# Last attention pair among the first state group's products, late sums one unit later, output projection by seven products

## The chip, the cores and the metric

One core of one Trainium2 chip runs the whole program in one launch. The metric is the device time of that core in microseconds, the median of several executions, lower is better. The kernel before takes 2818.53 us (three executions, 2817.77 to 2819.26).

## The reference

256 tokens of width 2048 (and 256 context tokens) pass two blocks. The first block has two layers, each with an RMS norm whose shift, scale and gate come from a small product of a condition vector with `ada_w` (2048 x 6144 per layer). What matters here is layer 0 and the norm behind it, cut to its lines:

```python
shift, scale, gate = adaln(c, ada_w[i], ada_b[i])
h = modulate(rms_norm(x, norm_g[i]), shift[:, None], scale[:, None])
p = h @ w_in                        # q, gate, z, k, v, and x, B, C, dt of the state space part
ya = neighbourhood_attention(q, k, v, kc, vc, rpb) * silu(gate_a)     # 16 heads
yb = gated_group_rmsnorm(bidirectional_ssd(lat, con, a) + d * x_lat, z, ssm_norm_g)   # 8 groups
out = concatenate([ya, yb]) @ w_out            # 4096 x 2048
x = x + gate[:, None] * out
```

All of it is float32. The second layer (a short convolution) and the second block (two more attentions) follow and are not touched, except that their first product waits for the norm of the new x.

## The kernel before, in words

Features lie on partitions: `hT` holds the normed tokens (256 own, 256 context) as 16 chunks of 128 features, `yT` the mixer's output, `xT` the residual. Weights come in tiles of 2048 rows by 256 columns (2 MB) into four slots `w[0..3]`, requested by SyncE in program order (`load`), each once `acc_full` says that TensorE has finished with the slot.

**Stages.** (1) Eight attention pairs (two heads each, `na(i)`), (2) eight state groups (`ssd(g)`), (3) the output projection (`out`) in eight tiles of 256 columns, then the next norm and the `sc` phase of layer 1.

**Seven products.** A tile's product is a 2 x 2 block product (two halves of the 2048 features, two halves of columns, two halves of tokens). Most phases do it with seven block products in place of eight (Strassen-Winograd): VectorE makes sums of token quarters once (`token_sums`) and of weight quarters for each tile (`sums_one` and `sums_two` in the attention, `weight_sums` from `sc` on: four subtractions of 128 x 1024 each), TensorE makes 7 x 8 matmuls of 128 x 128 instead of 16 x 2 of 128 x 256, ScalarE copies the seven blocks from PSUM to `staged`, and VectorE puts them together in six small additions (`na_combine`, `combine`). The state groups and the output projection use plain products. There `out_half` multiplies the first half of `yT` (the attention's output, the 2048 rows of weight slot 2*cb) or the second (slot 2*cb+1) into `bank[cb]`; `add_out` adds the bank, times the gate, to `xT`.

**A pair.** TensorE's program (`na` in the tensor block, L737) has six units of seven products each (`na_unit`: q, gate, k, k of the context, v, v of the context), and between them the scores, transposes and values of the pair before, a = i - 1 (`na_scores`, `na_transposes`, `na_values`), and three sums of squares (`na_sums`). Every engine runs its own program in order, so a wait holds up all that stands behind it.

**Late parts and late sums.** What `ada_w` still has to give (the gate of layer 0, all of layer 1) is computed beside the pairs. GpSimd fetches 1 MB pieces into a ring of two places (`late_chunks`; piece c is requested when VectorE has taken piece c - 2), VectorE multiplies and adds each into `aacc` (`late_part(i, c)`, four instructions of 128 x 512, eight parts per pair), then TensorE adds up the partitions with eight two-column matmuls (`late_sums(i)`, the last thing of a pair, waits for `late_taken` of all eight parts), and VectorE takes them into `mod` (`late_mod`).

**The last pair.** Its scores, transposes and values have no next pair to lie in: they stand by themselves after `na(7)` (TensorE, for h in range(2)), with softmax and transposed copies on VectorE between. The position biases of pair 7 (`na_biases(7)`: four small gathers on SyncE, a mask addition on VectorE, L1767) are requested inside `ssd(0)`, behind the loads of slots 0 and 1. Then comes `ssd(0)`: X in two column halves (`featured(..., 0, 0)` and `(..., 0, 1)`, 16 matmuls of 512 columns each), between them `steps_of_dt` (64 matmuls of 64 columns), then `sums_of_dt`, B, C, Z and the transposes.

The order of each engine's program is written out by hand.

## Time and profile before

| | us |
|---|---|
| median of three executions | 2818.53 |
| the profiled execution, its own time | 2821.06 |
| its span in the trace | 2818.9 |
| TensorE matmul busy | 2734.9 (97%) |
| TensorE weight load busy | 2363.3 |
| VectorE busy | 1548.2 (55%) |
| ScalarE busy | 466.4 (17%) |
| mean of what the DMA queues moved | 160 GB/s |

The page gives busy time per engine over the span. A matmul of the program shows as two records in the trace (float32), so a product of eight matmuls is x16 there. PEclk is the granted TensorE clock as a share of 2.4 GHz: 0.50 is 1.2 GHz. "idle before <- releaser" tells how long the engine stood still before an instruction and what ended that.

### The profile page before, as it was taken

Reading aid. Unit: us, or ns where it says so; the run is one execution under the profiler, and the core shown is the slowest. Engines: PE = TensorE matmul, PEld = TensorE weight load, DVE = VectorE, ACT = ScalarE, POOL = GpSimd, SP = SyncE. Lnnn points to the kernel's source line nnn. Section 1 sums busy time; section 2 is a strip of 40 time slices with the busy share of each in tenths; the row PEclk is TensorE's granted clock in tenths of the full one; section 3 lists DMA queues with packets and bytes.
Section 4 is the critical chain, followed back from the end, with each engine's and each line's share of the span. In section 5 each row is a group of like instructions: output and inputs, shape, how many; then the busy total and the mean of one; then the engine's idle time right before and its main releaser. Section 6 shows DMA issues by size and latency. Waiting matters only on the chain. (4 is left out here: it accounts for less than half of the span.)

```text
span 2818.9 us, 44137 instructions
## 1 busy us (share of the span) xinstructions
PE 2734.9 (97%) x18608; PEld 2363.3 (84%) x18608; DVE 1548.2 (55%) x2733; ACT 466.4 (17%) x915; POOL 51.2 (2%) x72
## 2 busy tenths in 40 slices
PE   7999999999996999999999999999999999999999
PEld 1498999999995666666668888999999899999999
DVE  3686676776673245555554004565666665555543
ACT  0221111121211122222221001111111111121211
POOL 0000000000000000000000000000000000000000
PEclk9999999999997999999999999999999999999999
DMA  9765665566545233333333554555554544445442
GB/s 383 284 201 166 201 203 180 175 219 194 169 135 174 73 105 105 104 104 104 104 104 105 179 168 149 162 180 161 166 178 158 172 148 139 144 150 160 157 137 87
DMA packets 380515, 450.07 MB, mean 160 GB/s; under 512 B 20452, under 2 KB 351704, under 8 KB 379480
## 3 DMA queue, kind: packets, MB, share of 16 engines
q1 hardware_dynamic: 351232, 354.86, 40.0%
q0 software_dynamic: 19520, 75.50, 7.5%
q10 hardware_dynamic: 9624, 17.68, 1.7%
q8 instruction: 109, 1.79, 0.3%
q14 instruction: 30, 0.25, 0.0%
HBM read 441.66 MB, written 6.36 MB: 159 GB/s over the span
## 5 line engine op out<-in xcount | busy, mean ns | idle before, releaser
L556 PE MATMUL bank<-hT,w 128*128 128x128 f32 (+2 forms) x6144 | 1017.9, 324 | 6.1 <-ACT hT L1200 4.6
L556 PEld LDWEIGHTS bank<-hT,w 128*128 128x128 f32 x6144 | 801.1, 195 | 191.6 <-issue 181.9
L556 PE MATMUL bank<-yT,w 128*128 128x128 f32 (+1 forms) x3872 | 569.8, 308 | 1.7 <-DVE yT L2038 1.0
L556 PEld LDWEIGHTS bank<-yT,w 128*128 128x128 f32 x3872 | 531.3, 191 | 33.4 <-DVE yT L2038 1.2
L1200 ACT ACTIVATE work<-bank 128x512 f32<-128x512 f32 (+2 forms) x298 | 153.9, 525 | 1210.6 <-PE bank L556 1205.7
L556 PE MATMUL bank<-hT,work 128*128 128x128 f32 x2352 | 279.5, 275 | 0.0
L556 PEld LDWEIGHTS bank<-hT,work 128*128 128x128 f32 x2352 | 270.9, 192 | 0.0
L556 PEld LDWEIGHTS bank<-w,hT 128*128 128x128 f32 x1792 | 245.0, 191 | 20.8 <-issue 5.7
L556 PE MATMUL bank<-w,hT 128*128 128x128 f32 (+2 forms) x1792 | 261.4, 305 | 0.7 <-DMA work<-in_ssd_d 0.7
L1782 DVE SCALAR_TENSOR_TENSOR work<-xT,silc,work 128x512 f32<-128x512 f32 x240 | 180.4, 752 | 76.9 <-DMA xT<-in_ada_w 69.8
L1200 ACT ACTIVATE work<-work 128x512 f32<-128x512 f32 (+3 forms) x299 | 168.5, 569 | 275.7 <-DVE work L1935 150.3
L556 PE MATMUL bank<-work 128*128 128x256 f32 (+2 forms) x400 | 118.0, 416 | 23.5 <-issue 18.7
L556 PEld LDWEIGHTS bank<-w,yT 128*128 128x128 f32 x1024 | 116.9, 192 | 3.8 <-issue 3.8
L2093 DVE TENSOR_TENSOR work<-yT 128x128 f32<-128x128 f32 x37 | 10.8, 293 | 195.8 <-ACT yT L1200 195.8
L556 PE MATMUL bank<-w,yT 128*128 128x128 f32 x1024 | 118.2, 275 | 0.0
L2093 DVE TENSOR_TENSOR work<-work 128x128 f32<-128x128 f32 x40 | 11.7, 292 | 170.8 <-ACT work L1200 170.8
L556 PEld LDWEIGHTS bank<-work 128*128 128x128 f32 x400 | 71.1, 196 | 34.3 <-issue 22.1
L2118 DVE SCALAR_TENSOR_TENSOR xT<-bank,mod,xT 128x256 f32<-128x256 f32 x16 | 7.0, 480 | 166.3 <-PE bank L556 166.3
L1935 DVE SCALAR_TENSOR_TENSOR work<-work,colp 128x512 f32<-128x512 f32 (+1 forms) x128 | 87.6, 685 | 15.1 <-DVE work L1933 0.9
L2081 DVE TENSOR_TENSOR w<-w 128x1024 f32<-128x1024 f32 x77 | 94.3, 1225 | 2.6
L556 PE MATMUL bank<-w,work 128*2 128x512 f32 (+1 forms) x192 | 76.0, 551 | 9.8 <-DMA w<-in_ada_w 9.8
L1933 DVE TENSOR_SCALAR work<-work,colp 128x512 f32<-128x512 f32 (+1 forms) x32 | 16.3, 510 | 115.1 <-ACT work L1200 115.1
(190 smaller groups left out, 2224.2 us busy)
## 6 DMA issues: line engine op xcount, KB each, us to landing
w<-in_na_ssd_w_in SPq DMA_DIRECT2D x48, 2048.0 KB, 11.0
xT<-in_ada_w POOLq DMA_DIRECT2D x64, 1024.0 KB, 7.5
w<-in_sc_w_in SPq DMA_DIRECT2D x32, 2048.0 KB, 9.0
w<-in_w_in SPq DMA_DIRECT2D x32, 2048.0 KB, 9.0
w<-in_na_ssd_w_out SPq DMA_DIRECT2D x16, 2048.0 KB, 10.0
w<-in_ada_w SPq DMA_DIRECT2D x12, 2048.0 KB, 11.3
w<-in_na_ssd_w_in SPq DMA_DIRECT2D x16, 1024.0 KB, 7.7
w<-in_sc_w_out SPq DMA_DIRECT2D x8, 2048.0 KB, 8.6
```

Source lines behind the costliest of these rows:

```text
L556: return nc.tensor.matmul(dst, lhsT, rhs, start=start, stop=stop, skip_group_check=free)
L1200: return nc.scalar.activation(*args, **kw)
L1782: last = v.scalar_tensor_tensor(out=aacc[:, block, :], in0=aring[:, at, kc, :], scalar=silc[:, k:k + 1], in1=aacc[:, block, :], op0=ALU.mu ...
L1933: link(v.tensor_scalar(o, tap(0), col("conv_w0", c), col("conv_b", c), ALU.mult, ALU.add))
L1935: last = v.scalar_tensor_tensor(out=o, in0=tap(k), scalar=col(f"conv_w{k}", c), in1=o, op0=ALU.mult, op1=ALU.add)
L2081: v.tensor_tensor(quarter(s, 0, 1), quarter(s, 1, 1), quarter(s, 0, 1), ALU.subtract)
L2093: v.tensor_tensor(u[:, 0, :], p(0), p(2), ALU.add)
L2118: last = v.scalar_tensor_tensor(out=chunk(xT, k + ch), in0=bank[b % 2][:, ch * T:(ch + 1) * T], scalar=gate, in1=chunk(xT, k + ch), op0=AL ...
```

## The change

1. The last pair's attention (pair 7) goes between halves of the first state group's two X products (TensorE's `ssd`, first iteration): scores of head 0, half of X's first column half, transposes, scores of head 1, the other half; values of head 0, transposes, late sums, half of X's second, values of head 1, the rest. `steps_of_dt` follows, and `sums_of_dt` moves between the two halves of B.
2. `na_biases(7)` is requested right after the last attention weight; the weights of dt are loaded by ScalarE right after its `na(7)` with a semaphore of their own.
3. `late_sums(a)` moves from the end of pair a to behind unit 0 of the next pair; VectorE does parts 6 and 7 of a pair at the start of the next one, around `sums_two(n + 1)`, and the others each a little later.
4. Output tiles 2 to 7 are made by seven products for each half of `yT`, added up in the same PSUM blocks over both halves. VectorE makes eight token sums and eight weight differences per tile (`out_sums`), ScalarE stages seven blocks (`staging_out`), VectorE combines them (`out_combine`). Tiles 0 and 1 stay plain products, but go through ScalarE's copy. The squares for the norm get a place of their own. The weight sums of the `sc` phase's slot 1 move behind the token sums.

```diff
--- before
+++ after
@@ -241,9 +241,10 @@
+    squared = L(2, 2, T)
...
-    assert u_pad.shape and 7812 <= WORK - 3 * 8 * P
+    assert u_pad.shape and 8836 <= WORK - 3 * 8 * P
@@ -276,7 +277,7 @@
-    PHASES = [("na", 8, 12, [2, 4, 8, 12]), ("ssd", 8, 6, [2, 4, 6, 6]), ("out", 4, 2, [1, 1, 2, 2]),
+    PHASES = [("na", 8, 12, [2, 4, 8, 12]), ("ssd", 8, 6, [2, 4, 6, 6]), ("out", 4, 4, [2, 2, 4, 4]),
@@ -312,6 +313,11 @@
+    OUT_IN = (lambda a, k: halves(yT, 0, a, k), lambda a, k: halves(yT, DC, a, k))
+    OUT_SUM = [{j: hT[:, EIGHT * (n // 2):EIGHT * (n // 2 + 1), T * h + (n % 2) * P:T * h + (n % 2 + 1) * P]
+                for n, j in enumerate((1, 2, 3, 4))} for h in range(2)]
@@ -480,6 +487,7 @@
+        na_biases(7)
@@ -740,6 +746,7 @@
+                late_sums(a)
@@ -757,19 +764,13 @@
-            late_sums(i)
...
-        for h in range(2):
-            na_scores(7, h)
-            na_transposes(7, h)
-            na_values(7, h)
...
-            pe.wait_ge(ssd_in, 64)
+            pe.wait_ge(wdt_in, 16)
@@ -802,20 +803,30 @@
             dst = accumulate("ssd", 0, g)
-            featured(dst[:, :], 0, 0, T + TC).then_inc(acc_full, 1)
             if first:
+                na_scores(7, 0)
+                featured(dst[:, :], 0, 0, T + TC, None, range(EIGHT))
+                na_transposes(7, 0)
+                na_scores(7, 1)
+                featured(dst[:, :], 0, 0, T + TC, None, range(EIGHT, DC)).then_inc(acc_full, 1)
+                dst = accumulate("ssd", 1, g)
+                na_values(7, 0)
+                na_transposes(7, 1)
+                late_sums(7)
+                featured(dst[:, :], 0, 1, T + TC, None, range(EIGHT))
+                na_values(7, 1)
+                featured(dst[:, :], 0, 1, T + TC, None, range(EIGHT, DC)).then_inc(acc_full, 1)
                 steps_of_dt()
             else:
+                featured(dst[:, :], 0, 0, T + TC).then_inc(acc_full, 1)
                 pe.wait_ge(s_xtk, g)
...
                 last.then_inc(s_cb, 1)
-            dst = accumulate("ssd", 1, g)
-            featured(dst[:, :], 0, 1, T + TC).then_inc(acc_full, 1)
-            if first:
-                sums_of_dt()
-            else:
+                dst = accumulate("ssd", 1, g)
+                featured(dst[:, :], 0, 1, T + TC).then_inc(acc_full, 1)
                 pe.wait_ge(s_xe, g)
@@ -923,25 +936,44 @@
-        def out_proj(i):
...
+        for cb in range(2):
+            loaded(2 * cb + 1, "out", 0)
+            for ch in range(2):
+                last = out_half(cb, ch, 1)
+            last.then_inc(acc_full, 2)
+        def out_products(tile, half):
+            def add(dst, weights, tokens, clears):
+                for kc in range(EIGHT):
+                    last = mm(dst, weights[:, kc, :], tokens[:, kc, :], clears and half + kc == 0, half == 1 and kc == EIGHT - 1, True)
+                return last
+            s = 2 * (tile % 2) + half
+            pair = (bank[3], bank[4]) if tile % 2 == 0 else (bank[0], bank[1])
+            loaded(s, "out", tile // 2)
+            x, sums, (t1, t2, t4) = OUT_IN[half], OUT_SUM[half], [(sums_x, sums_y)[half][:, m, :, :] for m in range(3)]
+            a = lambda m: pair[0][:, m * P:(m + 1) * P]
+            b = lambda m: pair[1][:, m * P:(m + 1) * P]
+            if half == 0 and tile > 2:
+                pe.wait_ge(acc_free, BANKS["out"] + 2 * tile - 2)
+            add(a(0), quarter(s, 0, 0), x(0, 0), True)
+            add(a(1), quarter(s, 1, 0), x(0, 1), False)
+            pe.wait_ge(s_made, 12 + 4 * half)
+            pe.wait_ge(o_t, 2 * tile + half - 3)
+            add(a(3), quarter(s, 0, 1), sums[3], False)
+            last = add(a(2), t2, sums[2], False)
+            if half == 1:
                 last.then_inc(acc_full, 1)
-        iterations(pe, 4, out_proj)
+            add(b(0), t1, sums[1], True)
+            add(b(1), quarter(s, 1, 1), sums[4], False)
+            last = add(b(2), t4, x(1, 1), False)
+            last.then_inc(acc_full if half == 1 else o_half, 1)
+        for tile in range(2, 8):
+            for half in range(2):
+                out_products(tile, half)
         norm_halves(1)
@@ -1343,6 +1375,7 @@
+        act.dma_start(wdt, w_in[:, :, COL_DT:COL_DT + NDT]).then_inc(wdt_in, 16)
@@ -1469,17 +1501,39 @@
+        def staging_out(t):
+            flat = staged.rearrange("p a b -> p (a b)")
+            at = BANKS["out"] + 2 * t
+            wait(act, x_new, t)
+            if t < 2:
+                act.wait_ge(acc_full, at + 2)
+                A(flat[:, 0:4 * P], bank[t][:, :], ACT.Copy).then_inc(acc_free, 2)
+            else:
+                banks = (bank[3], bank[4]) if t % 2 == 0 else (bank[0], bank[1])
+                act.wait_ge(acc_full, at + 1)
+                A(flat[:, 0:4 * P], banks[0][:, :], ACT.Copy).then_inc(acc_free, 1)
+                act.wait_ge(acc_full, at + 2)
+                A(flat[:, 4 * P:7 * P], banks[1][:, 0:3 * P], ACT.Copy).then_inc(acc_free, 1)
...
-            for t in range(8):
-                act.wait_ge(acc_free, BANKS["out"] + t + 1)
-                square(t)
+            for t in range(9):
+                if t < 8:
+                    staging_out(t)
+                if t > 0:
+                    act.wait_ge(x_new, t)
+                    if t == 1:
+                        square(0)
+                    else:
+                        A(squared[:, (t - 1) % 2, :, :], xT[:, 2 * t - 2:2 * t, :], ACT.Square).then_inc(norm_sq, 1)
...
-                    act.wait_ge(x_new, t)
+                    act.wait_ge(x_new, 8 + t)
@@ -1857,12 +1911,14 @@
-                late_mod(a)
...
-                late_part(i, 0)
+                late_part(a, 6)
...
+                late_part(a, 7)
...
+            if not first:
+                late_mod(a)
@@ -1870,35 +1926,32 @@
-            if first:
-                late_part(i, 0)
-            else:
+            if not first:
...
-            late_part(i, 1)
+            late_part(i, 0)
...
+            late_part(i, 1)
+            sums_two(n + 3)
...
-            sums_two(n + 3)
-            late_part(i, 3)
...
+            late_part(i, 3)
...
-            late_part(i, 5)
...
-            late_part(i, 6)
-            late_part(i, 7)
+            late_part(i, 5)
@@ -1910,11 +1963,15 @@
+        late_part(7, 6)
+        na_softmax(7, 0, link)
+        late_part(7, 7)
+        na_turned(7, 0)
+        na_softmax(7, 1, link)
+        na_out(7, 0)
+        na_turned(7, 1)
...
-        for h in range(2):
-            na_softmax(7, h, link)
-            na_turned(7, h)
-            na_out(7, h)
+        na_out(7, 1)
@@ -2098,35 +2155,59 @@
-        def add_squares(t, squares):
+        def add_squares(t, squares, src=None):
...
-            return v.tensor_tensor(both, both, hT[:, ds(2 * t, 2), 0:T], ALU.add)
-        def add_out(phase, n, layer, squares):
...
+            return v.tensor_tensor(both, both, hT[:, ds(2 * t, 2), 0:T] if src is None else src, ALU.add)
+        def out_sums(tile, half):
+            s, place = 2 * (tile % 2) + half, (sums_x, sums_y)[half]
+            dve.wait_ge(w_loaded[s], loads(s, "out", tile // 2))
+            if half == 0 and tile > 2:
+                dve.wait_ge(o_half, tile - 2)
+            link(v.tensor_tensor(place[:, 0, :, :], quarter(s, 0, 1), quarter(s, 0, 0), ALU.subtract))
+            v.tensor_tensor(quarter(s, 0, 1), quarter(s, 1, 1), quarter(s, 0, 1), ALU.subtract)
+            link(v.tensor_tensor(place[:, 1, :, :], quarter(s, 1, 1), place[:, 0, :, :], ALU.subtract))
+            v.tensor_tensor(place[:, 2, :, :], quarter(s, 1, 0), place[:, 1, :, :], ALU.subtract).then_inc(o_t, 1)
+        def out_combine(t):
+            dve.wait_ge(acc_free, BANKS["out"] + 2 * t + 2)
+            p = lambda n: staged[:, n, :]
+            v.tensor_tensor(partial[:, 0, :], p(0), p(2), ALU.add)
+            link(v.tensor_tensor(u_b[:, 0, 0:P], p(0), p(1), ALU.add))
+            link(v.tensor_tensor(partial[:, 1, :], partial[:, 0, :], p(3), ALU.add))
+            v.tensor_tensor(u_b[:, 1, :].rearrange("p (a b) -> p a b", a=2), partial,
+                            p(4).unsqueeze(1).broadcast_to([P, 2, P]), ALU.add)
+            link(v.tensor_tensor(u_b[:, 0, P:T], partial[:, 1, :], p(6), ALU.add))
+            v.tensor_tensor(u_b[:, 1, 0:P], u_b[:, 1, 0:P], p(5), ALU.add).then_inc(o_c, 1)
+            dve.wait_ge(o_c, t - 1)
+        def add_out():
+            first = staged.rearrange("p a b -> p (a b)")
+            for t in range(8):
+                if t >= 2:
+                    if t < 7:
+                        out_sums(t + 1, 0)
+                    else:
+                        dve.wait_ge(o_half, 6)
+                        weight_sums("sc", 0, 0, link)
+                    out_combine(t)
...
-                    body(i, link)
-            add_squares(7, squares).then_inc(norm_sum, 1)
+                    dve.wait_ge(acc_free, BANKS["out"] + 2 * t + 2)
+                for ch in range(2):
+                    k = 2 * t + ch
+                    gate = mod[:, 0, 2 * DC + k:2 * DC + k + 1, 0:1].rearrange("p a b -> p (a b)")
+                    last = v.scalar_tensor_tensor(out=chunk(xT, k), in0=u_b[:, ch, :] if t >= 2 else first[:, ch * T:(ch + 1) * T],
+                                                  scalar=gate, in1=chunk(xT, k), op0=ALU.mult, op1=ALU.add)
+                last.then_inc(x_new, 1)
+                dve.wait_ge(x_new, t + 1)
+                if t == 0:
+                    out_sums(2, 0)
+                if t >= 2:
+                    link(add_squares(t - 1, 2, squared[:, (t - 1) % 2, :, :]))
+                if 1 <= t < 7:
+                    out_sums(t + 1, 1)
+            add_squares(7, 2, squared[:, 1, :, :]).then_inc(norm_sum, 1)
@@ -2147,7 +2228,10 @@
-        add_out("out", 4, 0, 2)
+        token_sums(OUT_IN[0], OUT_SUM[0], (0, EIGHT), link)
+        dve.wait_ge(s_y, 16)
+        token_sums(OUT_IN[1], OUT_SUM[1], (0, EIGHT), link)
+        add_out()
@@ -2158,6 +2242,7 @@
+        weight_sums("sc", 0, 1, link)
```

**TensorE, end of pair 6 and start of pair 7** (`work` is attention data and the late parts' `aacc`, `hT` and `yT` tokens and their sums, `w` weights). Before:

```order
L556 MATMUL bank<-w,hT 128x128 x8
L556 MATMUL bank<-cst,work 128x2 x8
L556 MATMUL bank<-hT,w 128x128 x16
L556 MATMUL bank<-yT,w 128x128 x32
L556 MATMUL bank<-hT,w 128x128 x8
L556 MATMUL bank<-work 128x512
L556 MATMUL bank<-work,cst 128x256
```

Changed:

```order
L562 MATMUL bank<-w,hT 128x128 x8
L562 MATMUL bank<-hT,w 128x128 x16
L562 MATMUL bank<-yT,w 128x128 x32
L562 MATMUL bank<-hT,w 128x128 x8
L562 MATMUL bank<-cst,work 128x2 x8
L562 MATMUL bank<-work 128x512
L562 MATMUL bank<-work,cst 128x256
```

The late sums (128x2 x8) have moved behind the 56 matmuls of unit 0.

**VectorE, the same place**: the bias mask (128x768), weight sums (128x1024, 128x8x128), late parts (`work<-xT,silc`) and `na_combine` of unit 0 (first row 128x128). Before:

```order
L1767 TENSOR_TENSOR work<-work,cst 128x768
L1793 TENSOR_TENSOR mod<-bank,colp 128x8
L1815 TENSOR_TENSOR w<-w 128x1024
L1816 TENSOR_TENSOR w<-w 128x8x128
L1780 TENSOR_SCALAR work<-xT,silc 128x512
L1782 SCALAR_TENSOR_TENSOR work<-xT,silc,work 128x512 x3
L1823 TENSOR_TENSOR w<-w 128x1024
L1825 TENSOR_TENSOR w<-w 128x1024
L1839 TENSOR_TENSOR work<-work 128x128
```

Changed:

```order
L1821 TENSOR_TENSOR work<-work,cst 128x768
L1869 TENSOR_TENSOR w<-w 128x1024
L1870 TENSOR_TENSOR w<-w 128x8x128
L1836 SCALAR_TENSOR_TENSOR work<-xT,silc,work 128x512 x4
L1877 TENSOR_TENSOR w<-w 128x1024
L1879 TENSOR_TENSOR w<-w 128x1024
L1836 SCALAR_TENSOR_TENSOR work<-xT,silc,work 128x512 x4
L1893 TENSOR_TENSOR work<-work 128x128
```

One late part (0 of the new pair) stood here; now two of the old pair (6 and 7) do.

**TensorE, last attention pair and the first state group** (`hT,w 128x512` is X, `wide<-cst,work` transposes, `w,hT 128x64` dt). Before:

```order
L559 MATMUL wide<-cst,work 128x128 x8
L556 MATMUL bank<-work 128x256 x4
L556 MATMUL bank<-work 128x512
L556 MATMUL bank<-work,cst 128x256
L556 MATMUL bank<-work 128x512
L556 MATMUL bank<-work,cst 128x256
L559 MATMUL wide<-cst,work 128x128 x8
L556 MATMUL bank<-work 128x256 x4
L556 MATMUL bank<-hT,w 128x512 x16
L556 MATMUL bank<-w,hT 128x64 x64
L556 MATMUL bank<-hT,w 128x512 x16
```

Changed:

```order
L562 MATMUL bank<-hT,w 128x512 x8
L565 MATMUL wide<-cst,work 128x128 x8
L562 MATMUL bank<-work 128x512
L562 MATMUL bank<-work,cst 128x256
L562 MATMUL bank<-work 128x512
L562 MATMUL bank<-work,cst 128x256
L562 MATMUL bank<-hT,w 128x512 x8
L562 MATMUL bank<-work 128x256 x4
L565 MATMUL wide<-cst,work 128x128 x8
L562 MATMUL bank<-cst,work 128x2 x8
L562 MATMUL bank<-hT,w 128x512 x8
L562 MATMUL bank<-work 128x256 x4
```

Each softmax now has half an X product (8 matmuls) beside it; before, nothing stood between scores and transposes.

## Rows read from the trace of the kernel before

**Rows 1.** The page: chain that ended last, shares of the span by line.

```profile
PE bank L556 42%; PE wide L556 4%; PE wide L559 0%; ACT hT L1200 0%; ACT work L1200 0%; ACT rs L1200 0%; DVE ssq L2104 0%; DVE xT L2136 0%; DVE xT L2118 0%; DVE yT L2038 0%; DVE hT L2200 0%; DVE hT L2153 0%; DVE w L1988 0%; PE bank L559 0%; DVE work L2344 0%
```

**Rows 2.** Windows: stretch, length, busy PE, PEld, DVE, ACT, POOL, PEclk, DMA, GB/s.

```profile
222.36:318.80 96.44, 93.28 (x743) 89.08 (x743) 64.48 (x107) 16.57 (x32) 5.98 (x8) 0.96 0.56 179
318.80:411.92 93.12, 93.12 (x742) 89.09 (x743) 64.48 (x107) 16.07 (x31) 5.98 (x8) 0.96 0.57 185
411.92:501.77 89.85, 89.85 (x744) 85.83 (x743) 66.41 (x108) 16.56 (x32) 6.74 (x9) 1.00 0.62 204
...
873.00:917.69 44.69, 18.73 (x66) 12.24 (x64) 10.80 (x23) 3.61 (x9) 0.00 (x0) 0.66 0.51 150
...
1500.00:1600.00 100.00, 96.11 (x460) 83.40 (x459) 26.86 (x73) 8.54 (x17) 0.00 (x0) 1.00 0.43 141
```

**Rows 3.** Timeline, TensorE: late sums that waited (start, length, ..., idle before, releaser).

```profile
222.36 2.26 PE L556 MATMUL bank<-cst,work 128*128 128x2 f32 x16 [3.84 <-DVE work L1782]
318.80 3.06 PE L556 MATMUL bank<-cst,work 128*128 128x2 f32 x16 [3.15 <-DVE work L1782]
...
684.27 3.27 PE L556 MATMUL bank<-cst,work 128*128 128x2 f32 x16 [2.42 <-DVE work L1782]
779.88 3.31 PE L556 MATMUL bank<-cst,work 128*128 128x2 f32 x16 [2.32 <-DVE work L1782]
```

**Rows 4.** Timeline, VectorE: from the end of a pair to the next.

```profile
594.21 1.41 DVE L1906 SCALAR_TENSOR_TENSOR work<-work,colp 128x512 f32<-128x512 f32 x2
595.53 0.28 DVE L1839 TENSOR_TENSOR work<-work 128x128 f32<-128x128 f32 x1
...
597.37 0.96 DVE L1767 TENSOR_TENSOR work<-work,cst 128x768 f32<-128x768 f32 x1
598.25 0.16 DVE L1793 TENSOR_TENSOR mod<-bank,colp 128x8 f32<-128x8 f32 x1
598.33 1.21 DVE L1815 TENSOR_TENSOR w<-w 128x1024 f32<-128x1024 f32 x1
...
600.72 0.48 DVE L1780 TENSOR_SCALAR work<-xT,silc 128x512 f32<-128x512 f32 x1
```

**Rows 5.** Timeline, ScalarE: staging in the `sc` phase, one seven-product tile apart.

```profile
1781.36 0.49 ACT L1200 ACTIVATE work<-bank 128x384 f32<-128x384 f32 x1 [4.76 <-PE bank L556]
...
1793.86 0.49 ACT L1200 ACTIVATE work<-bank 128x384 f32<-128x384 f32 x1 [4.76 <-PE bank L556]
```

**Rows 6.** Timeline, VectorE and GpSimd: a late part that waits for its piece, five pairs.

```profile
312.48 6.27 DVE L1782 SCALAR_TENSOR_TENSOR work<-xT,silc,work 128x512 f32<-128x512 f32 x8 [7.78 <-DMA xT<-in_ada_w]
...
493.46 6.27 DVE L1782 SCALAR_TENSOR_TENSOR work<-xT,silc,work 128x512 f32<-128x512 f32 x8 [2.15 <-DMA xT<-in_ada_w]
...
571.95 0.75 POOL L418 DMA_DIRECT2D xT<-in_ada_w  x1 [7.05 <-DVE work L1782]
...
585.50 6.27 DVE L1782 SCALAR_TENSOR_TENSOR work<-xT,silc,work 128x512 f32<-128x512 f32 x8 [4.20 <-DMA xT<-in_ada_w]
...
677.58 3.12 DVE L1782 SCALAR_TENSOR_TENSOR work<-xT,silc,work 128x512 f32<-128x512 f32 x4 [6.78 <-DMA xT<-in_ada_w]
...
773.56 6.27 DVE L1782 SCALAR_TENSOR_TENSOR work<-xT,silc,work 128x512 f32<-128x512 f32 x8 [7.05 <-DMA xT<-in_ada_w]
```

**Rows 7.** Timeline, TensorE: a wait in the last state group.

```profile
1502.69 1.13 PE L556 MATMUL bank<-work 128*128 128x256 f32 x4 [1.65 <-DVE work L2064]
```

**Rows 8.** Timeline: bias request and mask of pair 7, sums of squares, dt.

```profile
858.78 1.02 PE L556 MATMUL bank<-work,cst 128*128 128x512 f32 x2
...
876.02 5.93 SPq L472 DMA_DIRECT2D work<-in_na_rpb  x4
...
892.48 0.96 DVE L1767 TENSOR_TENSOR work<-work,cst 128x768 f32<-128x768 f32 x1 [16.94 <-DMA work<-in_na_rpb]
...
932.48 14.51 PE L556 MATMUL bank<-w,hT 128*128 128x64 f32 x128 [0.68 <-DMA work<-in_ssd_d]
```

**Rows 9.** Timeline: output projection, TensorE, its last six tiles and the norm behind it.

```profile
1569.30 166.00 PE L556 MATMUL bank<-yT,w 128*128 128x256 f32 x768 [0.75 <-issue]
...
1737.73 1.13 PE L556 MATMUL bank<-ssq,cst 128*128 128x256 f32 x4 [2.42 <-DVE ssq L2104]
```

More of the change, by code:

```diff
@@ L1000, in sc @@
                 if is_first(i) and s == 0:
-                    seven("sc", s, i, H, H_SUM, (norm_out, 2 * DC), 8)
+                    seven("sc", s, i, H, H_SUM, (norm_out, 2 * DC), 16)
                 else:
@@ L1077, in sbreak @@
             if first:
-                seven("sb", 0, i, H, H_SUM, (norm_out, 3 * DC), 20)
+                seven("sb", 0, i, H, H_SUM, (norm_out, 3 * DC), 28)
             else:
@@ L1179, in rows @@
             last.then_inc(o_tr, 1)
-        pe.wait_ge(s_made, 32)
+        pe.wait_ge(s_made, 40)
         for t in range(2, 7):
@@ L2099, in combine @@
             dve.wait_ge(c_made, TILES[phase] + 4 * i + s + 1)
-        def add_squares(t, squares):
+        def add_squares(t, squares, src=None):
             dve.wait_ge(norm_sq, squares + t + 1)
             both = ssq[:, :].rearrange("p (a b) -> p a b", a=2)
-            return v.tensor_tensor(both, both, hT[:, ds(2 * t, 2), 0:T], ALU.add)
-        def add_out(phase, n, layer, squares):
-            per = PHASE[phase][2]
-            def body(i, link, ahead=None):
-                for b in range(per):
-                    if ahead and b == 1:
-                        ahead(0)
-                        ahead(1)
-                    k = i * (2 * per) + 2 * b
-                    dve.wait_ge(acc_full, BANKS[phase] + i * per + b + 1)
-                    for ch in range(2):
-                        gate = mod[:, layer, ds(2 * DC + k + ch, 1), 0:1].rearrange("p a b -> p (a b)")
-                        last = v.scalar_tensor_tensor(out=chunk(xT, k + ch), in0=bank[b % 2][:, ch * T:(ch + 1) * T],
-                                                      scalar=gate, in1=chunk(xT, k + ch), op0=ALU.mult, op1=ALU.add)
-                    last.then_inc(acc_free, 1)
-                    if not (isinstance(i, int) and i * per + b < 2):
-                        link(add_squares(i * per + b - 1, squares))
-            for i in range(n):
-                if i == n - 1:
-                    body(i, link, lambda b: weight_sums("sc", 0, b, link))
-                else:
-                    body(i, link)
-            add_squares(7, squares).then_inc(norm_sum, 1)
```

29 lines of the change are left out of this document (7 added, 22 removed).

## The prediction

> **What bounds the kernel now.** I read the page first, then the windows of the attention pairs, then the waits of TensorE, then the timeline around each wait. The chain that ended last runs almost wholly through TensorE's matmul line [rows 1], so an edit is worth what it takes from TensorE's program: matmul time, waits, or time at the lower clock. VectorE, ScalarE and the queues count only where TensorE waits for them. The reader is to see three places. First, seven attention pairs of the same work last 89.85 us when nothing disturbs them, and 93.12 or 96.44 otherwise [rows 2]. Second, the stretch after the last pair is 44.69 us long and TensorE is busy for 18.73 of it, at a mean clock of 0.66 [rows 2]. Third, the output projection is plain: its last six tiles are 768 records in 166.00 us [rows 9], 27.67 us a tile, while a seven-product tile of one weight slot takes 12.50 us (two stagings of the same form are 12.50 apart [rows 5]), which is 25.0 for the two slots of an output tile.
>
> **How the sum is made.** The profiled execution took 2821.06 us, its span is 2818.9; the median shown is 2818.53. All terms are differences read in that one execution, and I take them from the median.
>
> **Output projection.** Tiles 2 to 7 save 27.67 - 25.00 = 2.67 us each, 16.0 us in six. VectorE's new work per tile is eight subtractions of some 1.22 (as in rows 4), 9.8, with a combination of 1.84 (595.53 to 597.37 [rows 4]), additions of 0.9 and squares of 0.7: 13.3 us beside 25 of TensorE. Differences for the first half of tile t+1 are made when half 0 of tile t is done (12.5 us before they are wanted), those for the second after tile t's combination, some 9 us into tile t+1, wanted at 16. Both are covered, by 3 us or more; without that cover each missing microsecond would be paid once per tile. ScalarE gains two copies a tile, far below its limit. Tile 2 now needs only one slot to start, where TensorE waited 0.75 us for two [rows 9]: -0.75. Behind the last tile comes a copy (0.49 and a hop, 0.6) and a combination (1.84) before the additions: +2.4. This wait is already there (2.42 [rows 9]) and ends in a low clock either way. The weight sums of `sc` slot 1, now behind the token sums, take 4.9 us, while TensorE has its own last product of slot 0 and two of slot 1 (3 x 1.79 = 5.4) to do: nothing. Sum: **-14.3**. Bounds: with every difference in time and a free tail -16.7; if each tile still waits, 0.
>
> *A page weighed here.* By the rows a 256-column record costs 166.00/768 = 0.216 us and a 128-column one 12.50/112 = 0.1116. The Trainium skill ("TensorE: Matmul & The Clock Gate", section "Wait — 56ns, not 53.3ns?") puts a fixed 2.5 ns or so on every matmul, which speaks against seven small products in place of wide ones. Estimated from that page, the ratio of 128 to 256 columns is 55.8 to 109.2 ns, a tile would save 2.9 us and six 17.6; the rows show slightly more loss, and they decide.
>
> **The last attention pair.** The stretch of 44.69 us holds the late sums, two scores, two sets of transposes and two values. What these cost at full clock follows from the clean pair: 89.85 less six units of 12.50 and three sums of squares of at most 1.02 [rows 8] leaves 11.8. So 32.9 us are waits and low clock. The biggest wait goes because the biases are requested a pair earlier: now the gathers are issued at 876.02 and the mask waits 16.94 us for them [rows 8]. What is late next is the mask itself. VectorE has, after the last unit, the staging copy and hop (0.6), the combination (1.84) and the mask (0.88, 597.37 to 598.25 [rows 4]), so TensorE waits 3.3 us before its first scores. I count a fall of the clock for that: 3.3 us more (price below). Each softmax then lies beside half an X product of about 7 us (16 records of 512 columns, four times 128 x 0.1116 each: 7.1), and VectorE needs about 3 for a softmax plus 3.1 for the late part before or behind it; head 1's values stand behind another such half. Moving dt's weights ahead takes its 0.68 us [rows 8]. The sums of dt now lie inside B; their own short wait and low clock remain. Term: -32.9 + 3.3 + 3.3 - 0.7 = **-27.0**, with bounds of -31 (the clock holds, mask sooner) and -20 (half a softmax exposed twice).
>
> **Late sums one unit later.** Now TensorE waits at four of eight late sums, 3.84 + 3.15 + 2.42 + 2.32 = 11.7 us [rows 3]. After each the clock is at 1.2 GHz for a while: a pair without a wait but after one lasts 93.12 against 89.85, 3.27 more, and 96.44 - 3.15 - 89.85 gives 3.44 [rows 2, 3]. With 3.35 a time the four cost 13.4; together **25.1 us** that the move could give back.
>
> But what stands behind it? VectorE's order at the start of a pair, from TensorE's last matmul of the pair before: 0.6 (copy and hop), 1.84 (combination), 0.88 (mask), 2.39 (first weight sums, 598.33 to 600.72 [rows 4]), 3.12 (part 6, the x4 row [rows 6]), 2.4 (second weight sums), 3.12 (part 7). That is 14.4 us. TensorE reaches the late sums after one unit, 12.5. So it waits 1.9 us in each of seven pairs, even if VectorE is in time for all that went before. The old order hid this: the late sums ended one pair and two parts had been finished before it.
>
> VectorE is not in time. The piece for old part 6 lands 3.2 us before the end of its pair (312.48 against 318.80 - 3.15 [rows 6, 3]), or 8.3, 6.1, 4.3 and 4.0 before it in the other rows (493.46 against 501.77, 585.50 against 501.77 + 89.85, 677.58 against 681.85, 773.56 against 777.56 [rows 2, 3, 6]). It was requested when part 4 was taken; new part 5 is requested when part 3 is, at the same place in the pair, beside the same loads and gathers. Behind it now come its own 3.12, 2.4 of weight sums and 1.4 for k [rows 4], 6.9 us, before the pair's last combination, which could start 0.6 after the end. A piece that lands less than 6.3 before the end delays the chain: by 3.1, 0, 0.2, 2.0 and 2.3 us, mean 1.5. The wait becomes 1.9 + 1.5 = 3.4, seven times: 23.8.
>
> Does the clock fall? It did after each wait of 2.32 and more followed by the late sums [rows 3], in which the array does almost nothing; a wait of 1.65 before wide matmuls left it at 1.00 [rows 2, 7]. New waits lie between 1.9 and 5, also followed by late sums. I take six falls in seven: 20.1. Bounds: none, 0; seven, 23.5. New cost 43.9, less 25.1: **+18.8** (from -11.8 with seven waits of 1.9 and no fall, to +32 with 4.8 and seven falls).
>
> Sum: -14.3 - 27.0 + 18.8 = -22.5, so 2796 us.
>
> **Rivals.**
> (a) *Pieces come early* (0.15). Part 5 lands with time to spare, waits are 1.9 and the clock falls in five pairs: 13.3 + 16.8 - 25.1 = +5, total -36.3, 2782 us. For it: two of five landings would do it. Against it: the piece requested at 571.95 is used at 585.50, 13.6 us later, with VectorE idle for it [rows 6].
> By the Trainium skill ("DMA: Bandwidth & Descriptors", section "Anatomy of one DMA — SWDGE (gpsimd) path"), such a transfer takes about 2.0 us plus its bytes over 436 GB/s, an estimated 4.4 us for 1 MB, which would make this rival the forecast; the trace does not agree here, with 13.6 where other queues move data as well.
> (b) *The clock holds* (0.10): waits of 1.9, no fall. -11.8 in the pairs, 2765 us. For it: 1.9 is nearer to 1.65 than to 2.42. Against it: the 1.84 us of late sums behind each.
> (c) *The interleaved softmaxes are exposed* (0.08): VectorE meets late part 7 before it copies the transposes, and its order lets each head wait some 3 us, with a fall each: 2 x (3 + 3.3) = +12.6, 2809 us. For it: a late part of 3.1 stands in front. Against it: 7 us of X beside each.
> (d) *Seven products bring nothing* (0.05), because slots arrive late (two loads must land, then 4.9 us of differences, inside one tile of 25) and each tile waits 2.7 us: 2812 us. Against it: VectorE is busy for 26.86 of the 100 us in which this phase begins [rows 2].
> (e) *Slower* (0.05). VectorE's lateness at the pair's start feeds on itself: part 5's piece arrives in all pairs 3.6 us later than in the mean row, so that the wait before the late sums is 7 us. Seven times 7 + 3.35 = 72.5, less 25.1, is +47.4 against gains of 41.3: 2825 us. It decides from a wait of (41.3 + 25.1)/7 - 3.35 = 6.1 us on. Against it: the longest that the rows give is 1.9 + 3.1 = 5.0.
>
> **How the numbers follow.** The forecast has 0.57; its own range is 2786 to 2806. Below 2772 lies rival (b), above 2811 lie (e) and parts of (c) and (d), some 0.17 together: range 2772 to 2811. About 0.2% of this kernel (5.6 us) is what a measurement can tell from no change. Faster by more, under 2812.9: 0.89. Within it: 0.06. Slower: 0.05.
>
> **What would show it.** In the new trace: late sums (128x2) with an idle time before them of 1.9 to 5 us in all seven pairs and windows of pairs at 0.95 to 0.97 clock, pairs of 95 to 98 us; VectorE's part 7 as the releaser. One wait of some 3.3 us before the first scores of pair 7, then no idle over 1 us until dt; dt's matmuls begin some 47 us behind the last unit (3.3 + 11.8 + 28.6 of X + 3.3 for the clock = 47), with both X products already done. Output tiles 25.0 us apart with TensorE idle nowhere between. I am wrong if the late sums don't wait (then 2752), if pairs are shorter than 92 us, or if output tiles are above 26.

## The result, and the profile after

| | before | after |
|---|---|---|
| median of the runs (four of each) | 2818.15 | 2800.9 |
| lowest and highest | 2816.86, 2819.26 | 2798.93, 2804.05 |
| the profiled execution's own time, its span | 2821.06, 2818.9 | 2804.05, 2801.8 |
| PE busy, DVE busy, ACT busy | 2734.9, 1548.2, 466.4 | 2726.5, 1625.3, 473.9 |

The ratio is 0.9946, 95% interval 0.9929 to 0.9963: faster by 17.2 us (forecast: 22.5 faster, 2796 us, range 2772 to 2811). In the traces the change gains 41.3 us in two places and gives 24.2 of them back in the third, in waits that it lengthens and in the lower clock behind them.

The page follows the chain that ended last through the whole span, and the chain passes through VectorE and a DMA (first two lines, after). Before's page (third line) can't be set beside it: there the chain was followed back only to 1518 us, 46% of the span, so [rows 1] says nothing of the attention pairs.

```profile
PE 88%; DVE 7%; DMA 4%; issue 1%; ACT 0%; SPq 0%; DVEq 0%; POOLq 0%; ACTq 0%
PE bank L562 81%; PE wide L562 5%; DMA xT<-in_ada_w 3%; DVE work L1836 3%; DMA w<-in_ada_w 1%; PE wide L565 1%; DVE w L1877 1%; DVE w L1869 1%; DVE w L1870 1%; DVE w L1879 1%; PE bank L565 0%; DVE work L1959 0%; ACT work L1232 0%; DVE work L1896 0%; DVE work L1895 0%
```

```profile
PE 45%; DVE 0%; ACT 0%; issue 0%; DVEq 0%; ACTq 0%
```

**Late sums.** TensorE's timeline after, which answers to [rows 3]; where four of eight late sums waited before, seven do:

```profile
236.72 3.57 PE L562 MATMUL bank<-cst,work 128*128 128x2 f32 x16 [5.63 <-DVE work L1836]
334.13 3.57 PE L562 MATMUL bank<-cst,work 128*128 128x2 f32 x16 [3.68 <-DVE work L1836]
433.14 3.57 PE L562 MATMUL bank<-cst,work 128*128 128x2 f32 x16 [4.51 <-DVE work L1836]
529.51 2.18 PE L562 MATMUL bank<-cst,work 128*128 128x2 f32 x16 [1.88 <-DVE work L1836]
623.81 3.57 PE L562 MATMUL bank<-cst,work 128*128 128x2 f32 x16 [2.59 <-DVE work L1836]
719.90 1.95 PE L562 MATMUL bank<-cst,work 128*128 128x2 f32 x16 [3.06 <-DVE work L1836]
815.23 3.57 PE L562 MATMUL bank<-cst,work 128*128 128x2 f32 x16 [3.60 <-DVE work L1836]
```

The waits sum to 25.0 us (11.7 before). A pair ends 12.5 us, one unit, before such a wait begins: at 218.59, 317.95, 416.13, 515.13 and so on. The windows between these ends answer to [rows 2]; the columns are the same, and the granted clock, 1.00 in an undisturbed pair, is below it in each:

```profile
218.59:317.95 99.36, 93.72 (x744) 88.38 (x744) 66.35 (x109) 16.68 (x32) 6.74 (x9) 0.95 0.54 176
317.95:416.13 98.18, 94.50 (x744) 88.93 (x744) 63.66 (x106) 16.68 (x32) 5.24 (x7) 0.95 0.56 179
416.13:515.13 99.00, 94.49 (x744) 88.92 (x744) 67.71 (x110) 16.67 (x32) 6.75 (x9) 0.95 0.56 184
515.13:608.72 93.59, 91.71 (x744) 86.82 (x744) 63.20 (x105) 16.68 (x32) 5.99 (x8) 0.98 0.57 181
```

Length less wait less 89.85 (the undisturbed pair) is what the clock took: 3.88, 4.65, 4.64 and 1.86 in these, 24.8 us in all seven.

**Last pair.** TensorE's timeline behind the last unit (ends 897.31) answers to the 44.69 us window [rows 2] and to [rows 8]:

```profile
900.93 2.05 PE L562 MATMUL bank<-work 128*128 128x512 f32 x2 [3.62 <-DVE work L1821]
902.76 1.06 PE L562 MATMUL bank<-work,cst 128*128 128x256 f32 x2
...
906.18 7.21 PE L562 MATMUL bank<-hT,w 128*128 128x512 f32 x16
913.22 1.04 PE L565 MATMUL wide<-cst,work 128*128 128x128 f32 x8
...
926.15 1.84 PE L562 MATMUL bank<-cst,work 128*128 128x2 f32 x16
...
943.39 14.40 PE L562 MATMUL bank<-w,hT 128*128 128x64 f32 x128
```

One wait for the mask (L1821), 3.62 us, then nothing idle up to dt, 46.1 us behind the last unit. The late sums without a wait take 1.84 us.

**Output projection.** ScalarE's staging copies stand 25.01 us a tile apart (27.67 before [rows 9]), and TensorE waits nowhere inside; the norm behind waits longer than its 2.42 [rows 9]:

```profile
1689.89 0.49 ACT L1232 ACTIVATE work<-bank 128x384 f32<-128x384 f32 x1 [4.70 <-PE bank L562]
...
1714.90 0.49 ACT L1232 ACTIVATE work<-bank 128x384 f32<-128x384 f32 x1 [4.70 <-PE bank L562]
```

```profile
1536.89 31.46 PE L562 MATMUL bank<-yT,w 128*128 128x256 f32 x160 [0.97 <-DVE yT L2095]
...
1719.66 2.07 PE L562 MATMUL bank<-ssq,cst 128*128 128x256 f32 x4 [4.80 <-DVE ssq L2161]
```

**Where the 17.1 us of span went,** by the same marks in both traces:

| stretch | before | after | difference | forecast |
|---|---|---|---|---|
| start to end of pair 0 | 218.52 | 218.59 | +0.1 | 0 |
| pairs 1 to 7 | 654.48 | 678.72 | **+24.2** | +18.8 |
| end of pair 7 to behind the sums of dt | 91.33 | 64.3 | **-27.0** | -27.0 |
| first matmul of the output projection to its norm | 197.07 | 182.77 | **-14.3** | -14.3 |
| all else | | | -0.1 | 0 |

(64.3 is 968.45 - 6.87 - 897.31: half of B, 6.87 us, now lies ahead of the sums of dt and is taken off.)

### The profile page after: what moved, and what is told of

The parts are those of the page before. It is cut to its first block, busy times and chain, and to the rows that moved or that the text cites. A ratio compares the mean times of both kernels' runs of the same rounds, so it can differ in the third digit from the quotient of the medians.

```text
span 2801.8 us, 45408 instructions
## 1 busy us (share of the span) xinstructions
PE 2726.5 (97%) x19184; PEld 2370.1 (85%) x19184; DVE 1625.3 (58%) x2825; ACT 473.9 (17%) x929; POOL 51.2 (2%) x72
## 2 busy tenths in 40 slices
DMA packets 380523, 450.19 MB, mean 161 GB/s; under 512 B 20452, under 2 KB 351704, under 8 KB 379480
## 3 DMA queue, kind: packets, MB, share of 16 engines
q1 hardware_dynamic: 351232, 354.86, 41.3%
## 4 chain that ended last, share of the span: by engine, by line
PE 88%; DVE 7%; DMA 4%; issue 1%; ACT 0%; SPq 0%; DVEq 0%; POOLq 0%; ACTq 0%
PE bank L562 81%; PE wide L562 5%; DMA xT<-in_ada_w 3%; DVE work L1836 3%; DMA w<-in_ada_w 1%; PE wide L565 1%; DVE w L1877 1%; DVE w L1869 1%; DVE w L1870 1%; DVE w L1879 1%; PE bank L565 0%; DVE work L1959 0%; ACT work L1232 0%; DVE work L1896 0%; DVE work L1895 0%
## 5 line engine op out<-in xcount | busy, mean ns | idle before, releaser
L562 PE MATMUL bank<-hT,w 128*128 128x128 f32 (+2 forms) x6528 | 1056.5, 320 | 6.1 <-ACT hT L1232 4.6
L562 PEld LDWEIGHTS bank<-hT,w 128*128 128x128 f32 x6528 | 838.5, 193 | 190.9 <-issue 180.6
L562 PE MATMUL bank<-yT,w 128*128 128x128 f32 (+1 forms) x3488 | 448.5, 288 | 1.0 <-DVE yT L2095 1.0
L562 PEld LDWEIGHTS bank<-yT,w 128*128 128x128 f32 x3488 | 429.4, 192 | 12.5 <-DVE yT L2095 1.2
L1232 ACT ACTIVATE work<-bank 128x512 f32<-128x512 f32 (+2 forms) x312 | 161.6, 526 | 1352.1 <-PE bank L562 1328.1
L562 PE MATMUL bank<-hT,work 128*128 128x128 f32 x2736 | 324.3, 275 | 0.0
L562 PEld LDWEIGHTS bank<-hT,work 128*128 128x128 f32 x2736 | 314.8, 192 | 0.0
L1836 DVE SCALAR_TENSOR_TENSOR work<-xT,silc,work 128x512 f32<-128x512 f32 x240 | 180.2, 751 | 49.2 <-DMA xT<-in_ada_w 42.4
L562 PE MATMUL bank<-work 128*128 128x256 f32 (+2 forms) x400 | 126.4, 437 | 5.3 <-DVE work L1821 3.6
L2150 DVE TENSOR_TENSOR work<-work 128x128 f32<-128x128 f32 x40 | 11.7, 292 | 166.3 <-ACT work L1232 166.3
L562 PEld LDWEIGHTS bank<-w,work 128*2 128x2 f32 (+1 forms) x192 | 23.3, 123 | 62.6 <-issue 56.3
L2137 DVE TENSOR_TENSOR work<-w 128x1024 f32<-128x1024 f32 x59 | 72.1, 1221 | 6.4 <-PE bank L562 3.6
## 6 DMA issues: line engine op xcount, KB each, us to landing
w<-in_sc_w_in SPq DMA_DIRECT2D x32, 2048.0 KB, 10.2
w<-in_ada_w SPq DMA_DIRECT2D x12, 2048.0 KB, 11.1
```

What stands on the lines that cost most here:

```text
L562: return nc.tensor.matmul(dst, lhsT, rhs, start=start, stop=stop, skip_group_check=free)
L1232: return nc.scalar.activation(*args, **kw)
L1836: last = v.scalar_tensor_tensor(out=aacc[:, block, :], in0=aring[:, at, kc, :], scalar=silc[:, k:k + 1], in1=aacc[:, block, :], op0=ALU.mu ...
L2137: link(v.tensor_tensor(t[:, 0, :, :], quarter(s, 0, 1), quarter(s, 0, 0), ALU.subtract))
L2150: v.tensor_tensor(u[:, 0, :], p(0), p(2), ALU.add)
```

## Experiments

Theory A is the prediction's: three terms, and VectorE's order at the start of a pair makes TensorE wait 1.9 us or more before the moved late sums, with a fall of the clock each time. Every kernel ran beside the one before on its chip (medians of 2818.3 to 2819.7 us there). The changed kernel was not run again beside them, so what is said "against the changed kernel" compares medians of different sessions (2800.9 beside 2818.15). Diffs are cut to the lines that matter.

**1. Output projection alone** (`out_only`: before with item 4 of the change).

> The kernel before with the output projection's part of the change alone (tiles 2 to 7 by seven products, two slots each). Theory A, that of the prediction: six tiles save 2.67 us each, 0.75 at the seam, 2.4 more behind the last tile: 14 us faster, 2804 us, tiles 25.0 us apart. Theory B, that the gain of the whole change is mostly made here and the rest cancels: 17 us or more. Theory C, the slots or differences come late: less than 8 us, with TensorE waits before the third product of a tile.

Measured: 2803.3 us, ratio 0.9942 (0.9925 to 0.9959), 15.6 faster. In its trace the phase runs from 1527.61 to 1710.38, 182.77 us, as in the changed kernel. The term of -14.3 stands alone. Rival (d), seven products bring nothing, falls.

The pairs of this kernel are those of before, and its trace shows what one execution's readings are worth: four late sums wait, but for 2.47, 1.33, 1.98 and 1.95, 7.7 us, where before's profile has 11.7 [rows 3].

**2. Last pair alone** (`pair_only`: before with items 1 and 2).

> The kernel before with the last attention pair laid among the first state group's X, its biases and dt's weights requested sooner; late sums as before, at the end of each pair. Theory A: 27 us faster, 2791 us; one wait of some 3.3 us before the first scores of pair 7 (the mask), the four waits of the old late sums stay. Theory B, the interleaving hides only part of it and the sooner late sums' move is harmless: 15 to 20 us faster, with waits over 1 us at the transposes.

Measured: 2785.3 us, ratio 0.9888 (0.9866 to 0.9911), 33.6 faster; A's 27 is missed by 6.6. TensorE's timeline:

```profile
874.82 2.01 PE L555 MATMUL bank<-work 128*128 128x512 f32 x2 [1.94 <-DVE work L1772]
914.42 14.40 PE L555 MATMUL bank<-w,hT 128*128 128x64 f32 x128
```

Pair 7 ends at 871.04, so the stretch up to dt is 43.4 us, 2.7 shorter than the 46.1 of the changed kernel: the late sums, still at the pair's end, are TensorE's work while VectorE makes the mask, and the wait is 1.94 and not 3.62. The rest lies in the pairs before (10.2 us of waits against 11.7, pair 7 ending 1.95 sooner) and in the spread of the runs (2783.4 to 2801.2). Six of its late sums waited, where A had four.

**3. Late sums alone** (`late_only`: before with item 3).

```diff
+                late_sums(a)          # behind unit 0 of the next pair
...
-            late_sums(i)              # at the end of pair i
```

> The kernel before with the late sums behind unit 0 of the next pair and parts 6 and 7 at its start, nothing else (parts 6 and 7 of the last pair stand before its mask). Theory A: TensorE waits 1.9 to 5.6 us before the late sums in each of seven pairs and the clock falls after most: 19 us slower, 2837 us. Theory B, the late sums' move costs as much as it gives back: within 6 us of before.

Measured: 2839.8 us, ratio 1.0085 (1.006 to 1.011), 20.9 slower. Waits in seven pairs: 5.51, 3.55, 3.29, 1.88, 3.39, 2.84, 3.50, sum 24.0. This part of the change costs by itself, as A says; the other two are not needed for it.

**4. The change with the late sums put back** (`late_old`).

> The changed kernel with the late sums and late parts put back as they were (end of each pair, parts 6 and 7 in their own pair). Theory A: the waits before the late sums go back from seven (25.0 us) to four (11.7 us) and three falls of the clock go: 19 us faster than the changed kernel, 2782 us. Theory B: no difference to the changed kernel beyond 4 us, 2797 to 2804.

Measured: 2771.6 us, ratio 0.9841 (0.9822 to 0.986), 29.3 faster than the changed kernel, where A said 19. The direction holds; the size is missed by 10. The two parts alone add up to the same kernel: 2818.9 - 15.6 - 33.6 = 2769.7. Its trace has four waits before late sums, 2.45, 2.54, 0.19 and 1.25, 6.4 us in all, and a mask wait of 1.94. Why its pairs wait 6.4 us, out_only's 7.7 and before's 11.7 with the same order in the pairs is not settled.

**5. Late sums behind the first scores** (`late_scores`, against the changed kernel).

```diff
-                late_sums(a)
                 na_scores(a, 0)
+                late_sums(a)
```

> The changed kernel with each pair's late sums behind the first scores of the pair before instead of ahead of them: 2.5 us of TensorE's work moves in front of the wait, nothing else changes. Theory A (each wait costs itself and, past some length, a fall of the clock of 3.35 us): the seven waits of 25.0 us shrink by 2.5 each to 7.7 us or so, none is over 3.2, some three falls remain instead of seven: 30 us faster than the changed kernel, 2771 us. Theory B (the clock does not matter, only the waits do): 17 us faster, 2784 us. Theory C (VectorE's lateness just moves on and meets TensorE later): under 8 us.

Measured: 2769.6 us, ratio 0.9821 (0.9798 to 0.9844), 31.3 faster than the changed kernel. The scores put 2.6 us of TensorE's work in front of the wait (842.61 to 845.19 in the trace of experiment 7); five waits are left (3.31, 2.35, 1.28, 0.93, 1.21), 9.1 us in all. In the traces the pairs are 27.2 us shorter, 15.9 of them waits and 11.3 clock (4.1 more lie before the end of pair 0, as in experiment 6): A's 30 holds, not B's 17.

**6. Late sums behind unit 1** (`late_unit1`), with VectorE's `late_mod` behind that unit's combination.

```diff
-                late_sums(a)
                 na_scores(a, 0)
             na_unit(i, 1)
             if not first:
+                late_sums(a)
                 na_transposes(a, 0)
```

> The changed kernel with the late sums behind unit 1 of the next pair, and late_mod behind the combination of unit 1. VectorE's 14.4 us up to part 7 then have 27.5 us of TensorE's work beside them, so no wait before the late sums is left. Theory A: 25.0 us of waits and seven falls of 3.35 go, 48 us faster than the changed kernel, 2753 us, pairs of 89.9 us. Theory C (the lateness moves on): waits appear at the transposes or scores instead, over 2765 us.

Measured: 2750.1 us, ratio 0.9761 (0.9746 to 0.9776); one of its six executions took 5696.12 us and is left out of the ratio. The whole of the seven pairs, in a window of its trace, is TensorE busy without a gap at full clock:

```profile
215.00:842.50 627.50, 627.50 (x5190) 599.20 (x5188) 450.80 (x742) 114.94 (x224) 42.51 (x57) 1.00 0.60 194
```

The changed kernel without the new wait is 50.8 us faster, what the waits and the clock took: 25.0 + 24.8 = 49.8. The two traces differ by 50.5 in the pairs, by 1.1 in the stretch behind them and by 4.3 before the end of pair 0 (218.59 against 214.33), where both run the same program: so much can one execution differ from another with nothing changed. The forecast had said 2752 "if the late sums don't wait".

**7. Mask sooner too** (`late_unit1_mask`, against `late_unit1`).

```diff
+            if i == 7:
+                na_biases(7)
             na_combine(i, 5, vtok[:, 2:4, :])
...
-        na_biases(7)
```

> As the kernel with late sums behind unit 1, and besides the mask of pair 7 added before the last combination of pair 7 instead of behind it (1.84 + 0.88 us sooner). Theory A: the wait of 3.6 us before the scores of pair 7 shrinks below 1 us and the clock does not fall there: 3 to 6.5 us faster than late_unit1. Theory B: values or scores wait for the combination instead, no difference.

Measured: 2743.9 us (2741.53 to 2746.76), ratio 0.9742 (0.9727 to 0.9758): 6.2 faster again, 74 under before, the fastest kernel here. TensorE goes from the last unit into the scores without a wait and is at dt 39.62 us later, against 45.0 in `late_unit1` (846.13 - 3.62 to 887.51):

```profile
842.61 1.02 PE L562 MATMUL bank<-work 128*128 128x512 f32 x2
...
882.23 14.40 PE L562 MATMUL bank<-w,hT 128*128 128x64 f32 x128
```

That makes this wait of 3.62 worth 5.4 us, 1.8 of them clock.

**8. Biases of pair 7 requested late** (`bias_late`: the changed kernel with the request at its old place, behind the first loads of the state groups).

> The changed kernel with the biases of pair 7 requested where they were before (SyncE, behind the loads of slots 0 and 1 of the first state group). Theory A: the early request is what makes the interleaving worth anything: TensorE stands some 17 to 19 us before the scores of pair 7 instead of 3.6, 14 to 15 us slower than the changed kernel, 2815 us. Theory B: the gathers land fast when issued alone, within 5 us of the changed kernel.

Measured: 2821.4 us, ratio 1.0012 (1.0 to 1.0023), 20.5 slower than the changed kernel, more than A's 14 to 15. The interleaved attention is worth little without the sooner request:

```profile
920.55 2.05 PE L563 MATMUL bank<-work 128*128 128x512 f32 x2 [22.35 <-DVE work L1822]
```

22.35 - 3.62 = 18.7 of it stand in this wait. TensorE's own wait for this mask was 18.69 in before's trace; here the late sums (1.84) no longer stand in front of it, and the four gathers take 7.78 us to issue against 5.93 [rows 8]: 18.69 + 1.84 + 1.85 = 22.4. A had left both out.

**9. Why the piece is late** (`few_packets`). The page of the changed kernel has VectorE waiting in seven places for the piece of part 5 (8.51, 6.56, 7.39, 2.08, 5.46, 5.93 and 6.47 us in its trace). One such case on GpSimd and VectorE: the piece requested at 589.21 is used at 603.12, 13.9 us later.

```profile
589.21 0.75 POOL L425 DMA_DIRECT2D xT<-in_ada_w  x1 [7.31 <-DVE work L1836]
```

```profile
603.12 3.12 DVE L1836 SCALAR_TENSOR_TENSOR work<-xT,silc,work 128x512 f32<-128x512 f32 x4 [5.46 <-DMA xT<-in_ada_w]
```

```diff
-                    src = bass.AP(ins["na_rpb"].tensor, at + h * 465 + (5 - (1 - half)) * 31 - 48,
-                                  [[1, NA_COLS], [31, 6], [1, NA_COLS]])
-                    sp.dma_start(hankel[half * 64:half * 64 + 64, h, :, :], src).then_inc(na_hk_in, 16)
+                    src = bass.AP(ins["na_rpb"].tensor, h * 465 + half * 31, [[1, NA_COLS], [1, 6 * NA_COLS]])
+                    dst = hankel[half * 64:half * 64 + 64, h, :, :].rearrange("p a b -> p (a b)")
+                    sp.dma_start(dst, src).then_inc(na_hk_in, 16)
```

> The changed kernel with the gathers of the relative position biases read as 64 rows of 384 numbers instead of 384 rows of 64 (the biases' values are other ones; every shape, wait and product stays). Theory A: the piece of the modulation's weights that the late part of unit 3 waits for lands late (VectorE waits 5 to 7 us for it in six pairs) because the small rows of the bias gathers stand ahead of it and slow it. Then the waits before the late sums, 25.0 us in seven pairs, go towards the 1.9 us of the pair whose piece came earliest, some 12 us less in all: about 2789. Rival B: the piece's lateness comes from the other large loads alone, or the small rows cost nothing beside them; then the waits stay at 25 us and the time within 3 us of the changed kernel's 2801.

Measured: 2783.5 us, ratio 0.9873 (0.9857 to 0.989), 17.4 faster than the changed kernel, where A had 12: in the traces the pairs are 13.6 us shorter, the stretch behind them is 2.8 shorter (its clock does not fall, see the last section), and 3.6 lie before the end of pair 0. By the page, packets under 512 B fall from 20452 to 8164, and the pieces' median from issue to landing from 7.3 to 5.7 us. VectorE's waits for part 5 (L1836) go from 42.4 us in seven to 0.2 us in one:

```profile
DVE work L1836 <- DMA xT<-in_ada_w: 42.4, 7, 8.5
```

```profile
DVE work L1836 <- DMA xT<-in_ada_w: 0.2, 1, 0.2
```

(the first is of the changed kernel, the second of this one; total, times, longest). And TensorE's late sums all wait alike:

```profile
324.60 2.76 PE L562 MATMUL bank<-cst,work 128*128 128x2 f32 x16 [1.88 <-DVE work L1836]
419.86 2.48 PE L562 MATMUL bank<-cst,work 128*128 128x2 f32 x16 [1.88 <-DVE work L1836]
515.12 2.19 PE L562 MATMUL bank<-cst,work 128*128 128x2 f32 x16 [1.88 <-DVE work L1836]
```

Seven waits of 1.88, 13.2 us, where there were 25.0. So the way in which the bias gathers are read makes the piece of part 5 late: rival B falls. That it is the length of the rows is likely but not shown, for the edit changes more: the four gathers of a pair take some 4 us to issue instead of 8 to 9, and they read other addresses, the same in every pair. VectorE's waits for the piece of part 4 stay as they were (L1834, 25.5 and 27.2 us in eight). What is left is VectorE's order, as the prediction added it up, and nothing waits in it once the copy of the last unit's blocks is there:

```profile
501.30 0.29 DVE L1893 TENSOR_TENSOR work<-work 128x128 f32<-128x128 f32 x1 [2.86 <-ACT work L1232]
...
503.14 0.96 DVE L1821 TENSOR_TENSOR work<-work,cst 128x768 f32<-128x768 f32 x1
504.02 1.22 DVE L1869 TENSOR_TENSOR w<-w 128x1024 f32<-128x1024 f32 x1
...
506.42 3.11 DVE L1836 SCALAR_TENSOR_TENSOR work<-xT,silc,work 128x512 f32<-128x512 f32 x4
509.56 1.23 DVE L1877 TENSOR_TENSOR w<-w 128x1024 f32<-128x1024 f32 x1
...
511.96 3.11 DVE L1836 SCALAR_TENSOR_TENSOR work<-xT,silc,work 128x512 f32<-128x512 f32 x4
```

The pair ends at 500.74 (515.12 - 1.88 - 12.5) and part 7 at 515.07: 14.3 us, against the 14.4 of the forecast. The interval from 419.86 to 515.12 is 95.26 us; less 1.88 and 89.85, the clock takes 3.53 behind a wait of 1.88. One wait that short costs 5.4 us; so it is in six of the seven pairs, and 3.8 us in the other (515.12 to 608.72, 93.60).

## Why the prediction was right, and where it was off

- **Bound by TensorE's program**: right, but the chain of [rows 1] doesn't show it: it covers 46% of the span and none of the pairs. The windows and the runs do. Every difference above is a wait of TensorE or time at the lower clock, apart from the products saved. VectorE's 77 us more of work cost nothing except where TensorE waited for it.
- **Output projection, -14.3**: -14.3 in the traces of two kernels. Six tiles at 25.01 us, and the norm's wait grew by 2.4 (2.42 to 4.80), both as added up. The six tiles save 6 x (27.67 - 25.01) = 16.0. The estimate by the Trainium skill ("TensorE: Matmul & The Clock Gate", section "Wait — 56ns, not 53.3ns?") had been 17.6; the rows hold.
- **Last pair, -27.0**: -27.0. The mask's wait is 3.62 instead of 3.3, the clock takes 2.8 (46.1 - 3.62 - 39.62 of the undisturbed stretch) instead of 3.3, and both softmaxes are covered; rival (c) falls. That it meets to the tenth is luck in part: these two errors have opposite signs, and the pair's own work is 11.1 (39.62 less 28.6 of X), not 11.8. Done alone it is worth more, by 2.7, since the late sums cover part of the mask.
- **Late sums, +18.8**: the mechanism was right, with its releaser, its least value of 1.9 (1.88) and its two parts. The term was too small by 5.4. The waits are 3.57 us in the mean and not 3.4 (+1.2). The forecast read how early the piece lands from five of the seven pairs before; with the two left out (used at 216.04, 2.5 us before its pair's end, shown below, and at 405.59, 6.3 before) its own sum gives 3.5. And the clock fell after all seven, where six were taken, and took 3.55 a time and not 3.35 (24.8 instead of 20.1, +4.7); what the old order gave back is 0.4 more (25.5), which leaves 5.5. Rival (a) describes `few_packets`, except that it had five falls and there are seven; rival (b) is shown wrong by the same run, where each wait of 1.88 had its fall.

```profile
216.04 6.26 DVE L1782 SCALAR_TENSOR_TENSOR work<-xT,silc,work 128x512 f32<-128x512 f32 x8 [8.21 <-DMA xT<-in_ada_w]
```

- **By medians the terms lie further apart**: -15.6 and -33.6 for the first two, each alone, and +29.3 for the late sums (the changed kernel against `late_old`). Together that is -19.9, near the 17.2 measured, but the last pair brings 6.6 more than forecast and the late sums cost 10.5 more. That the total is off by only 5 us is in part luck: these two errors have opposite signs.
- **Why the pieces are late** was left at "beside the same loads and gathers". Experiment 9 names the gathers, for part 5. By the Trainium skill ("DMA: Bandwidth & Descriptors", section "Anatomy of one DMA — SWDGE (gpsimd) path") such a piece of 1 MB needs an estimated 4.4 us; the trace's 7.3 in the median and 13.9 in this place do not agree, and without the small rows the median is still 5.7.
- **The median**: the profiled execution was the slowest of four, 3.2 above the median, before's was 2.9 above its own. In these two traces the 5.4 us by which the forecast was off (22.5 against 17.1) are the late sums'.
- The spread of the pairs was not in the forecast: the same order gave 6.4, 7.7, 10.2 and 11.7 us of waits in four traces. A term that is a sum of waits on a landing cannot be known better than that from one trace.

## What to carry over

Before a step is moved to "a unit later", add up on the engine that feeds it what stands between the last thing it needs and the new place, from the moment that frees that engine: here 14.4 us against 12.5, so the step waited in every turn, while one unit further it waited in none and was worth 51 us. Count each short wait in front of near-empty matmuls at its length and a fall of the clock, 5.4 us for 1.88 in most pairs here, and expect the fall to vary. And when a load that other engines hide is late, look at the form of the small loads beside it, not only at bytes.
